# Prompt stick-breaking attention: every one-minus row on GpSimd, a second scan buffer for wide rows, q/k/v loads on the SyncE queue

## Chip, core, metric
One core of one Trainium2 chip runs the whole program. The metric is the device time of one execution in microseconds (us). Three timed runs gave 3248.36 to 3249.91 us, median 3248.76 us.

## What is computed
A two-layer decoder step for 1024 prompt tokens and 64 sample tokens. The change lies in the prompt part of layer 1, stick-breaking attention with 12 heads of 64:

```
z         = q k^T / 8 + bias[head]          (strictly causal)
log_keep  = where(mask, log_sigmoid(-z), 0)
log_after = reverse_cumsum(log_keep) - log_keep
a         = where(mask, exp(log_sigmoid(z) + log_after), 0)
out       = a v
```

So with b = sigmoid(z), a weight is b at its key times the product of (1 - b) over all later keys up to the query.

## The kernel before
The kernel is written engine by engine, with explicit semaphores; each engine runs its instructions in the written order. Layer 1 runs in this order: projections, prompt memory attention, sample memory attention, **prompt stick-breaking attention** ("the stage" below), sample stick-breaking attention, output projection, feed-forward.

The stage takes six head pairs and, for each, eight blocks of 128 queries in the order 0, 7, 1, 6, 2, 5, 3, 4: 48 steps. Block t has (t+1)*128 key columns. Odd steps (blocks 7 to 4) are *wide*, 640 to 1024 columns; even steps are *narrow*, 128 to 512. Step s works on two heads (`hh`), so there are 96 head rows.

In a step:
- TensorE (`pe_bp`): scores of step s+2 into PSUM, then for each *fill* of two key blocks the transposes of step s's weights (`turn`) and the product with v of the fill before (`use`). Only two PSUM banks (4 and 5) take fills, so TensorE and ScalarE hand them back and forth.
- ScalarE (`act_bp`): `breaks(s + 2)`, the sigmoid of the scores into `brk_w` or `brk_n`; for wide steps also sigmoid(-z) into `left_w`, chunk by chunk. Then it copies the turned fills of step s out of PSUM to `brk_t`.
- VectorE (`dve_bp`): for a narrow row first one-minus (`tensor_scalar`, brk_n to left_n); for every row the running product (`tensor_tensor_scan`, two inputs in SBUF: the `left` row and a broadcast zero), then the product with the breaks (`tensor_tensor`, two inputs in SBUF). `copy_out` subtracts PSUM and SBUF for the low half of the result.
- GpSimd (`pool_bp`): issues the loads. `raw(i)` brings q and k of pair i from DRAM (2 x 512 KB) into `sb_raw`, `values(i)` its v into `sb_v`. It waits for the end of the sample memory attention (`ms_lo`) before the first.
- `prep(i, m)`: TensorE transposes a quarter of `sb_raw`, ScalarE copies it to `sb_qk`. Pair 0's four are done ahead of the steps; the others inside steps 1 to 4 of the pair before.

`sp_ms` loads keys and values of the sample memory attention on the SyncE queue; `sp_bs` loads pages for the next stage.

Of the kernel before, what the change touches and what calls it, by code (L numbers as in the profile page):

```python
# [68 lines left out]
def build(nc, A, O, scratch):  # L69
    es = ExitStack()  # L70
    with es:
# [81 lines left out]
        nbias12 = r("nbias12", [P, SH])  # L153
# [8 lines left out]
        sb_raw = r("sb_raw", [P, 2, NPT, P])  # L162
# [3 lines left out]
        left_w = r("left_w", [P, 2, SEQ + 1])  # L166
        left_n = r("left_n", [P, 2, 512 + 1])
# [685 lines left out]
        def sig_after(n, hh):  # L853

            count = 0
            for s in range(NSTEP):
                for m, _, _ in chunks(s):
                    if m == n:
                        return count + (2 if wide(s) else 1) * (hh + 1)
                    count += 4 if wide(s) else 2  # L860
# [30 lines left out]
        sb_v = sb_at("sb_v", [P, 2, NPT, P], w_hi_at + (2 + idle_half) * half)  # L891

# [3 lines left out]
        def left_edge(s):  # L896
            return (left_w, SEQ) if wide(s) else (left_n, 512)
# [7 lines left out]
        def pool_bp(pool):  # L905

            pool.wait_ge(ms_lo, 4)
            def raw(i):
                for n in range(2):
                    pool.dma_start(sb_raw[:, n, :, :], proj[0:SEQ, n * MIX + i * P:n * MIX + (i + 1) * P]  # L910
                                   .rearrange("(t p) f -> p t f", p=P)).then_inc(bp_ld, 16)

            def values(i):
                pool.dma_start(sb_v[:, i % 2, :, :], proj[0:SEQ, 2 * MIX + i * P:2 * MIX + (i + 1) * P]
                               .rearrange("(t p) f -> p t f", p=P)).then_inc(bp_v[i % 2], 16)
# [108 lines left out]
        def act_bp(act):  # L1024
# [36 lines left out]
            act.wait_ge(bp_one, 4)  # L1061
# [13 lines left out]
        def dve_bp(dve):  # L1075
            dve.wait_ge(ms_lo, 4)
            dve.memset(left_w[:, :, SEQ:SEQ + 1], 1.0).then_inc(bp_one, 1)
            dve.memset(left_n[:, :, 512:513], 1.0).then_inc(bp_one, 1)
            dve.memset(zero1[:, :], 0.0).then_inc(bp_one, 1)
            dve.wait_ge(bp_set, 16)  # L1080
            dve.tensor_scalar(nbias12[:, :], bias12[:, :], -1.0, None, ALU.mult).then_inc(bp_one, 1)
            dve.wait_ge(bp_one, 4)
# [6 lines left out]
            for s in range(NSTEP):  # L1089
# [1157 lines left out]
```

## Time and profile before

| | us |
|---|---|
| median of the timed runs | 3248.76 |
| the profiled execution | 3256.13 |
| its span, first to last instruction | 3254.6 |
| mean granted TensorE clock | 0.961 of full |
| the stage, end of sample memory attention to last result | 1717.5 to 2025.7 |

The profile describes one execution, 7.4 us above the median. Its page gives busy time by engine, the chain that ended last, and the costliest groups. Since the page is a mean over stages with different limits, the change is read in the stage's own window. "Idle before, releaser" is the time that an engine stood still ahead of a group, and whose semaphore ended it.

### The profile page before, as it was taken

How to read it: one execution, taken by the hardware profiler on the slowest of the kernel's cores; microseconds unless marked ns; L12 is line 12 of the kernel's file. 1: busy time of each engine (PE TensorE's matmuls, PEld its weight loads, DVE VectorE, ACT ScalarE, POOL GpSimd, SP SyncE). 2: the span in 40 equal slices, each digit the busy share in tenths (PEclk: the TensorE clock that was granted, in tenths of full speed). 3: DMA queues.
4: the chain of work that ended last, by engine and by line, in shares of the span. 5: the costliest groups of instructions: out<-in, count | busy, mean ns of one | idle time of the engine just before them, and what ended most of it. 6: DMA issues, size and time to landing. Idle time of an engine off the chain costs nothing.

```text
span 3254.6 us, 52029 instructions
## 1 busy us (share of the span) xinstructions
PE 3009.7 (92%) x20232; PEld 2669.0 (82%) x20232; DVE 1758.9 (54%) x2649; ACT 1077.6 (33%) x1794; POOL 92.8 (3%) x163
## 2 busy tenths in 40 slices
PE   6996799999999999899966887999999999999997
PEld 6994699999999999799944444556899999999996
DVE  4016225666666666610035777555335666666666
ACT  5223223222222222522245666454133222222221
POOL 0010000000000000000001000000000000000000
PEclk8998899999999999899978889999999999999998
DMA  4122211111111111122242111999311111111101
GB/s 135 48 96 78 63 39 33 39 53 44 39 39 39 58 39 39 56 75 80 80 135 62 32 34 37 357 390 390 120 33 40 39 45 51 39 39 39 58 26 67
DMA packets 188140, 260.61 MB, mean 80 GB/s; under 512 B 9560, under 2 KB 138222, under 8 KB 188044
## 3 DMA queue, kind: packets, MB, share of 16 engines
q1 hardware_dynamic: 170752, 197.23, 17.6%
q0 software_dynamic: 16512, 61.71, 6.0%
q8 instruction: 67, 1.10, 0.1%
q10 hardware_dynamic: 780, 0.34, 0.0%
q14 instruction: 29, 0.24, 0.0%
HBM read 238.24 MB, written 27.68 MB: 82 GB/s over the span
## 4 chain that ended last, share of the span: by engine, by line
PE 80%; ACT 6%; DVE 5%; DMA 4%; issue 2%; SPq 2%; ACTq 0%; POOL 0%; DVEq 0%; POOLq 0%
PE ps L320 23%; PE ps L321 23%; PE ps L322 22%; DMA pv_tail<-in_cache_sb_v_dram 2%; PE ps L994 2%; PE ps L429 2%; ACT brk_w L1041 1%; ACT left_w L1046 1%; DVE x L1966 1%; PE ps L979 1%; PE ps L1217 1%; PE ps L964 1%; PE ps L1256 1%; PE ps L1234 1%; ACT prob L1585 1%
## 5 line engine op out<-in xcount | busy, mean ns | idle before, releaser
L1966 DVE TENSOR_TENSOR x<-x,ps 128x512 f32<-128x512 f32 (+1 forms) x792 | 538.9, 687 | 305.7 <-PE ps L322 304.8
L320 PE MATMUL ps<-act_hi,w_hi 128*128 128x370 f32 x2112 | 702.3, 333 | 1.4 <-DVE act_lo L464 1.4
L321 PE MATMUL ps<-act_lo,w_hi 128*128 128x370 f32 x2112 | 701.4, 332 | 0.0
L322 PE MATMUL ps<-act_hi,w_lo 128*128 128x370 f32 x2112 | 699.6, 331 | 0.0
L320 PE MATMUL ps<-w_hi,act_hi 128*128 128x256 f32 (+1 forms) x1800 | 507.2, 282 | 3.4 <-DVE w_lo L316 2.0
L321 PE MATMUL ps<-w_lo,act_hi 128*128 128x256 f32 (+1 forms) x1800 | 506.6, 281 | 0.0
L322 PE MATMUL ps<-w_hi,act_lo 128*128 128x256 f32 (+1 forms) x1800 | 505.0, 281 | 0.0
L320 PEld LDWEIGHTS ps<-act_hi,w_hi 128*128 128x128 f32 x2112 | 398.7, 189 | 5.7 <-DVE act_lo L464 1.7
L321 PEld LDWEIGHTS ps<-act_lo,w_hi 128*128 128x128 f32 x2112 | 398.5, 189 | 2.0
L322 PEld LDWEIGHTS ps<-act_hi,w_lo 128*128 128x128 f32 x2112 | 397.9, 188 | 0.0
L316 DVE TENSOR_TENSOR w_lo<-w_raw,w_hi 128x2048 fp32r<-128x2048 f32 x73 | 167.3, 2292 | 357.2 <-ACT w_hi L312 357.2
L320 PEld LDWEIGHTS ps<-w_hi,act_hi 128*128 128x128 f32 (+1 forms) x1800 | 330.5, 184 | 4.3 <-DVE w_lo L316 2.5
L322 PEld LDWEIGHTS ps<-w_hi,act_lo 128*128 128x128 f32 (+1 forms) x1800 | 330.8, 184 | 0.0
L321 PEld LDWEIGHTS ps<-w_lo,act_hi 128*128 128x128 f32 (+1 forms) x1800 | 330.8, 184 | 0.0
L320 PE MATMUL ps<-d_hi,g_hi 128*128 128x512 f32 (+1 forms) x792 | 310.9, 393 | 17.9 <-DVE d_lo L1901 17.9
L321 PE MATMUL ps<-d_lo,g_hi 128*128 128x512 f32 (+1 forms) x792 | 310.1, 392 | 0.0
L322 PE MATMUL ps<-d_hi,g_lo 128*128 128x512 f32 (+1 forms) x792 | 309.9, 391 | 0.0
L1933 ACT ACTIVATE g_hi<-cv_u 128x1024 fp32r<-128x1024 f32 x44 | 46.6, 1060 | 610.0 <-DVE cv_u L1980 610.0
L312 ACT ACTIVATE w_hi<-w_raw 128x2048 fp32r<-128x2048 f32 x73 | 138.9, 1902 | 163.9 <-PE ps L322 142.4
L1923 ACT ACTIVATE up_g<-ps 128x1110 f32<-128x1110 f32 x44 | 48.3, 1098 | 431.1 <-PE ps L322 431.1
L320 PEld LDWEIGHTS ps<-d_hi,g_hi 128*128 128x128 f32 (+1 forms) x792 | 144.9, 183 | 50.8 <-issue 18.9
L322 PEld LDWEIGHTS ps<-d_hi,g_lo 128*128 128x128 f32 (+1 forms) x792 | 145.0, 183 | 36.6
(288 smaller groups left out, 3645.7 us busy)
## 6 DMA issues: line engine op xcount, KB each, us to landing
w_raw<-in_w_up_dram SPq DMA_DIRECT2D x88, 512.0 KB, 4.9
pk_w<-in_cache_sb_k_dram SPq DMA_DIRECT2D x64, 384.0 KB, 5.3
pv_w<-in_cache_sb_v_dram SPq DMA_DIRECT2D x64, 384.0 KB, 5.3
pk_tail<-in_cache_sb_k_dram SPq DMA_DIRECT2D x64, 384.0 KB, 5.5
pv_tail<-in_cache_sb_v_dram SPq DMA_DIRECT2D x64, 384.0 KB, 5.4
d_raw<-in_w_down_dram POOLq DMA_DIRECT2D x44, 512.0 KB, 3.8
projected<-stage POOLq DMA_DIRECT2D x13, 1024.0 KB, 5.2
w_raw<-in_w_in_b_dram SPq DMA_DIRECT2D x20, 512.0 KB, 4.3
```

The source lines that it names most:

```text
L312: act.activation(w_hi[:, par], w_raw[:, :, :], ACT.Copy).then_inc(wh_ok, 1)
L316: dve.tensor_tensor(w_lo[:, par], w_raw[:, :, :], w_hi[:, par].bitcast(F32), ALU.subtract).then_inc(w_ok, 1)
L320: pe.matmul(out, ahi, bhi, start=first, stop=False, **kw)
L321: pe.matmul(out, ahi, blo, start=False, stop=False, **kw)
L322: return pe.matmul(out, alo, bhi, start=False, stop=last, **kw)
L429: last = pe.matmul(out, src(t, k), diag[0:ROWS[t], t, 0:ROWS[t]], start=True, stop=True, skip_group_check=True)
L964: last = pe.matmul(ps[:, 2 * (n % 2) + hh, 0:w], sb_qk[i % 2][rows, 0, t * P:(t + 1) * P], sb_qk[i % 2][rows, 1, c0:c0 + w], start=True, s ...
L979: last = pe.transpose(ps[:, 4 + n % 2, c:c + P], breaks_of(s)[:, hh, kb * P:(kb + 1) * P], ident[:, :])
L994: last = pe.matmul(ps[hh * HD:(hh + 1) * HD, 6 + s // 2 % 2, s % 2 * P:(s % 2 + 1) * P], sb_v[:, i % 2, kb, hh * HD:(hh + 1) * HD], brk_t[ ...
L1923: act.activation(up[:, :].rearrange("p (g c) -> p g c", c=TG), src, ACT.Copy)
L1933: act.activation(g_hi[:, par, 0:SEQ], cv_u[:, 2:2 + SEQ], ACT.Copy).then_inc(gh_ok, 1)
L1966: dve.tensor_tensor(xs, xs, ps[0:ROWS[t], DN_BANK[(2 * t + c) % 4], :], ALU.add).then_inc(dn_ev, 1)
```

## The change
1. ScalarE no longer computes sigmoid(-z). VectorE no longer computes one-minus. GpSimd computes 1 - b for all 96 head rows, from the finished break row in SBUF, into `left_w` or `left_n`; VectorE's scan waits for it (`bp_keep`).
2. `left_w` has two buffers, so a wide row may be written while the one before is in use; `left_n` keeps one. `nbias12` goes.
3. q, k, v loads move to the SyncE queue. Those of pair 0 are issued between the loads of the sample memory attention; `sb_raw` moves to the place of `w_raw`. TensorE starts `prep(0, 0)` after `ms_ok`, without waiting for the masks.
4. Page table, bias and masks are set up by GpSimd after the prompt memory attention (`mq_lo`). The first page load of the next stage goes behind the last `prep`; the load of `qkn_raw` behind the last scores, since it now lies over `sb_qk0`.

The diff's core, in the order of the file: buffers, `sp_bp`, `pool_bp`, `pe_bp`, `act_bp` (in `breaks`), `dve_bp`, `sp_bs`. `first` is called in `sp_ms` behind `load(mvc[0], ...)`; `sig_after(n, hh)` is now 2n + hh + 1.

```diff
-        left_w = r("left_w", [P, 2, SEQ + 1])
-        left_n = r("left_n", [P, 2, 512 + 1])
+        left_w = r("left_w", [P, 2, 2, SEQ + 1])
+        left_n = r("left_n", [P, 1, 2, 512 + 1])
+        sb_raw = sb_at("sb_raw", [P, 2, NPT, P], w_hi_at + 4 * half)
...
+            def first():
+                sp.wait_ge(w_ok, out0[1] + 1)
+                sp.wait_ge(w_used, out0[1])
+                raw(0)
+                values(0)
...
-            pool.wait_ge(ms_lo, 4)
...
+            pool.wait_ge(mq_lo, 2 + 16)
...
+            pool.wait_ge(ms_lo, 4)
+            for s in range(NSTEP):
+                w = (step(s)[1] + 1) * P
+                left, end = left_edge(s)
+                for hh in range(2):
+                    pool.wait_ge(bp_sig, sig_after(chunks(s)[-1][0], hh))
+                    ago = 4 if wide(s) else 2
+                    if s >= ago:
+                        pool.wait_ge(bp_a, 2 * (s - ago) + hh + 1)
+                    pool.tensor_scalar(left[:, hh, end - w:end], breaks_of(s)[:, hh, 0:w], -1.0, 1.0, ALU.mult,
+                                       ALU.add).then_inc(bp_keep, 1)
...
-            pe.wait_ge(ms_lo, 4)
-            pe.wait_ge(masked, BP_MASKED)
+            pe.wait_ge(ms_ok, 4)
...
-                        if wide(s):
-                            if s >= 2:
-                                act.wait_ge(bp_a, 2 * (s - 2) + hh + 1)
-                            act.activation(left[:, hh, at + c0:at + c0 + w], z, ACT.Sigmoid, bias=nbias12[:, h:h + 1],
-                                           scale=-1.0).then_inc(bp_sig, 1)
...
-                    dve.wait_ge(bp_sig, sig_after(chunks(s)[-1][0], hh))
-                    if not wide(s):
-                        dve.tensor_scalar(c, row, -1.0, 1.0, ALU.mult, ALU.add).then_inc(bp_keep, 1)
-                        dve.wait_ge(bp_keep, s + hh + 1)
+                    dve.wait_ge(bp_keep, 2 * s + hh + 1)
...
+            sp.wait_ge(bp_z, chunks((NPAIR - 1) * NPT - 1)[-1][0] + 1)
```

ScalarE in the first pair, from the breaks of step 2 to the first fill of step 1, before:

```order
L1041 ACTIVATE brk_n<-ps,bias_83 128x256 x2
L1053 ACTIVATE brk_t<-ps 128x256
L1041 ACTIVATE brk_w<-ps,bias_83 128x384
L1046 ACTIVATE left_w<-ps,nbias_84 128x384
L1041 ACTIVATE brk_w<-ps,bias_83 128x384
L1046 ACTIVATE left_w<-ps,nbias_84 128x384
L1041 ACTIVATE brk_w<-ps,bias_83 128x512
L1046 ACTIVATE left_w<-ps,nbias_84 128x512
L1041 ACTIVATE brk_w<-ps,bias_83 128x512
L1046 ACTIVATE left_w<-ps,nbias_84 128x512
L1053 ACTIVATE brk_t<-ps 128x512 x4
L1029 ACTIVATE sb_qk_151<-ps 128x512
```

The same place of the changed kernel:

```order
L1054 ACTIVATE brk_n<-ps,bias_83 128x256 x2
L1060 ACTIVATE brk_t<-ps 128x256
L1054 ACTIVATE brk_w<-ps,bias_83 128x384 x2
L1054 ACTIVATE brk_w<-ps,bias_83 128x512 x2
L1060 ACTIVATE brk_t<-ps 128x512 x4
L1044 ACTIVATE sb_qk_149<-ps 128x512
```

Four of eight activations between the narrow breaks and the fills are gone.

VectorE at its first steps (scans are listed as SCALAR_TENSOR_TENSOR), before:

```order
L1098 TENSOR_SCALAR left_n<-brk_n 128x128
L1100 SCALAR_TENSOR_TENSOR left_n<-left_n,zero_90 128x128
L1103 TENSOR_TENSOR brk_n<-brk_n,left_n 128x128
L1098 TENSOR_SCALAR left_n<-brk_n 128x128
L1100 SCALAR_TENSOR_TENSOR left_n<-left_n,zero_90 128x128
L1103 TENSOR_TENSOR brk_n<-brk_n,left_n 128x128
L1100 SCALAR_TENSOR_TENSOR left_w<-left_w,zero_90 128x1024
L1103 TENSOR_TENSOR brk_w<-brk_w,left_w 128x1024
```

The changed kernel:

```order
L1102 SCALAR_TENSOR_TENSOR left_n<-left_n,zero_89 128x128
L1105 TENSOR_TENSOR brk_n<-brk_n,left_n 128x128
L1102 SCALAR_TENSOR_TENSOR left_n<-left_n,zero_89 128x128
L1105 TENSOR_TENSOR brk_n<-brk_n,left_n 128x128
L1102 SCALAR_TENSOR_TENSOR left_w<-left_w,zero_89 128x1024
L1105 TENSOR_TENSOR brk_w<-brk_w,left_w 128x1024
L1102 SCALAR_TENSOR_TENSOR left_w<-left_w,zero_89 128x1024
L1105 TENSOR_TENSOR brk_w<-brk_w,left_w 128x1024
```

and GpSimd, which had nothing but loads there, now runs these beside it, twelve of each width in all:

```order
L947 TENSOR_SCALAR left_n<-brk_n 128x128 x2
L947 TENSOR_SCALAR left_w<-brk_w 128x1024 x2
L947 TENSOR_SCALAR left_n<-brk_n 128x256 x2
L947 TENSOR_SCALAR left_w<-brk_w 128x896 x2
L947 TENSOR_SCALAR left_n<-brk_n 128x384 x2
L947 TENSOR_SCALAR left_w<-brk_w 128x768 x2
L947 TENSOR_SCALAR left_n<-brk_n 128x512 x2
L947 TENSOR_SCALAR left_w<-brk_w 128x640 x2
```

VectorE has only the scan and the product of each row left; every scan now stands behind one of these rows.

SyncE in the sample memory attention of layer 1, changed kernel (before, the two rows in the middle were on GpSimd, behind the page table's load):

```order
L1667 DMA mkc<-in_cache_mem_k_dram 128x2x256 x4
L1667 DMA mvc_123<-in_cache_mem_v_dram 128x2x256 x4
L896 DMA sb_raw<-projected 128x8x128 x2
L900 DMA sb_v<-projected 128x8x128
L1667 DMA mvc_124<-in_cache_mem_v_dram 128x2x256 x4
L1667 DMA mkc<-in_cache_mem_k_dram 128x2x256 x4
```

Pair 0's three loads stand ahead of the second half of the sample group's memory loads.

## Rows read from the trace of the kernel before

**Rows 1.** The page: busy time by engine, and the chain that ended last.
```profile
PE 3009.7 (92%) x20232; PEld 2669.0 (82%) x20232; DVE 1758.9 (54%) x2649; ACT 1077.6 (33%) x1794; POOL 92.8 (3%) x163
...
PE 80%; ACT 6%; DVE 5%; DMA 4%; issue 2%; SPq 2%; ACTq 0%; POOL 0%; DVEq 0%; POOLq 0%
```

**Rows 2.** Stretch, length, busy PE, PEld, DVE, ACT, POOL; clock, DMA share, GB/s.
```profile
1640.00:1690.00 50.00, 31.13 (x257) 23.48 (x256) 26.79 (x47) 27.19 (x85) 0.00 (x0) 0.84 0.37 119
1717.50:2025.70 308.20, 244.42 (x1776) 143.77 (x1777) 227.61 (x269) 201.00 (x410) 18.90 (x27) 0.88 0.12 35
```

**Rows 3.** Waits in the stage: who for whom, total us, times, longest.
```profile
PE ps L994 <- ACT brk_t L1053: 46.3, 29, 2.5
...
DVE left_n L1098 <- ACT brk_n L1041: 28.7, 14, 3.7
...
DVE left_w L1100 <- ACT left_w L1046: 20.1, 12, 3.2
...
DVE act_lo L1087 <- ACT act_hi L1057: 13.8, 12, 3.2
```

**Rows 4.** Groups in the stage: busy us, mean ns; idle before, releaser.
```profile
L1100 DVE TENSOR_TENSOR_SCAN left_w<-left_w,zero 128x1024 f32<-128x1024 f32 (+3 forms) x48 | 90.8, 1891 | 21.4 <-ACT left_w L1046 20.1
...
L1046 ACT ACTIVATE left_w<-ps,nbias 128x512 f32<-128x512 f32 (+3 forms) x96 | 60.2, 627 | 3.3 <-DVE brk_w L1103 3.3
...
L1103 DVE TENSOR_TENSOR brk_w<-brk_w,left_w 128x1024 f32<-128x1024 f32 (+3 forms) x48 | 49.2, 1025 | 1.6
L1100 DVE TENSOR_TENSOR_SCAN left_n<-left_n,zero 128x128 f32<-128x128 f32 (+3 forms) x48 | 39.6, 825 | 1.7
...
L1103 DVE TENSOR_TENSOR brk_n<-brk_n,left_n 128x128 f32<-128x128 f32 (+3 forms) x48 | 23.6, 492 | 1.6
...
L1098 DVE TENSOR_SCALAR left_n<-brk_n 128x128 f32<-128x128 f32 (+3 forms) x48 | 15.6, 326 | 29.1 <-ACT brk_n L1041 28.7
...
L1087 DVE TENSOR_TENSOR act_lo<-ps,act_hi 128x256 fp32r<-128x256 f32 x24 | 10.2, 425 | 14.2 <-ACT act_hi L1057 13.8
```

**Rows 5.** The chain into the stage: start, us, what.
```profile
1716.18 1.08 PE ps L1772 x4
...
1717.54 0.24 DVE act_lo L1715
...
1718.56 0.92 POOL sb_raw L910
1719.48 5.84 DMA sb_raw<-projected
...
1725.46 3.76 PE ps L951 x16
```

**Rows 6.** VectorE at the stage's start and end: start, us, what, idle before.
```profile
1732.48 0.33 DVE L1098 TENSOR_SCALAR left_n<-brk_n 128x128 f32<-128x128 f32 x1 [3.67 <-ACT brk_n L1041]
...
1736.17 2.29 DVE L1100 TENSOR_TENSOR_SCAN left_w<-left_w,zero 128x1024 f32<-128x1024 f32 x1 [1.52 <-ACT left_w L1046]
1738.50 1.22 DVE L1103 TENSOR_TENSOR brk_w<-brk_w,left_w 128x1024 f32<-128x1024 f32 x1
...
2018.01 0.82 DVE L1103 TENSOR_TENSOR brk_w<-brk_w,left_w 128x640 f32<-128x640 f32 x1
```

**Rows 7.** TensorE's last wide scores of the stage, in order of time.
```profile
2011.21 1.13 PE L964 MATMUL ps<-sb_qk 64*128 64x512 f32 x4
```

**Rows 8.** GpSimd's instructions that read and write SBUF, by form, whole execution.
```profile
L746 POOL TENSOR_SCALAR_AFFINE_SELECT w_raw<-w_raw 128x768 f32<-128x768 f32 x1 | 0.9, 876 | 4.8 <-DMA w_raw<-in_gm_v_norm_dram 4.8
...
L337 POOL TENSOR_SCALAR_AFFINE_SELECT ident<-ident 128x128 f32<-128x128 f32 x1 | 0.3, 282 | 0.2 <-POOL batch_of L331 0.2
```

**Rows 9.** Layer 0: GpSimd and VectorE at the same moment, in order of time.
```profile
239.30 0.88 POOL L746 TENSOR_SCALAR_AFFINE_SELECT w_raw<-w_raw 128x768 f32<-128x768 f32 x1 [4.82 <-DMA w_raw<-in_gm_v_norm_dram]
...
239.34 1.64 DVE L803 SCALAR_TENSOR_TENSOR v_all<-v_all,inv,w_raw 128x768 f32<-128x768 f32 x1 [12.21 <-DMA w_raw<-in_gm_v_norm_dram]
```

**Rows 10.** All of line 803: duration ns, minimum, median, maximum.
```profile
L803 DVE SCALAR_TENSOR_TENSOR v_all<-v_all,inv,w_raw x9: 1000/1008/1644, 239.3 to 247.4; 128x768 f32<-128x768 f32 x8, 64x768 f32<-64x768 f32 x1
```

More of the change, by code:

```diff
@@ L853, in sig_after @@
         def sig_after(n, hh):
[L855 to L860, printed above, removed]
+            return 2 * n + hh + 1
         def blocks(s, f):
@@ L896, in left_edge, with sp_bp, raw, values @@
         def left_edge(s):
-            return (left_w, SEQ) if wide(s) else (left_n, 512)
+            return (left_w[:, s // 2 % 2], SEQ) if wide(s) else (left_n[:, 0], 512)
+        def sp_bp(sp):
+            def raw(i):
+                for n in range(2):
+                    sp.dma_start(sb_raw[:, n, :, :], proj[0:SEQ, n * MIX + i * P:n * MIX + (i + 1) * P]
+                                 .rearrange("(t p) f -> p t f", p=P)).then_inc(bp_ld, 16)
+            def values(i):
+                sp.dma_start(sb_v[:, i % 2, :, :], proj[0:SEQ, 2 * MIX + i * P:2 * MIX + (i + 1) * P]
+                             .rearrange("(t p) f -> p t f", p=P)).then_inc(bp_v[i % 2], 16)
+            def first():
[3 more added lines that the diff above has]
+                values(0)
+            def rest():
+                for i in range(1, NPAIR):
+                    sp.wait_ge(bp_t, prep_no(i - 1, 3) + 1)
+                    raw(i)
+                    if i >= 2:
+                        sp.wait_ge(bp_av, av_after((i - 1) * NPT - 1))
+                    values(i)
+            return first, rest
         def pool_sb_out(pool):
@@ L905, in pool_bp @@
         def pool_bp(pool):
-            pool.wait_ge(ms_lo, 4)
[L908 to L915, printed above, removed]
+            pool.wait_ge(mq_lo, 2 + 16)
             pool.dma_start(page_t[:, :], A["page_table"].rearrange("b p -> (b p)").unsqueeze(0)).then_inc(bs_set, 16)
-            raw(0)
-            values(0)
             pool.dma_start(bias12[:, :], A["sb_bias"][0].partition_broadcast(P)).then_inc(bp_set, 16)
@@ L1033, in breaks @@
                 i, t = step(s)
-                left, end = left_edge(s)
-                at = end - (t + 1) * P
                 for n, c0, w in chunks(s):
@@ L1076, in dve_bp @@
             dve.wait_ge(ms_lo, 4)
-            dve.memset(left_w[:, :, SEQ:SEQ + 1], 1.0).then_inc(bp_one, 1)
-            dve.memset(left_n[:, :, 512:513], 1.0).then_inc(bp_one, 1)
+            dve.memset(left_w[:, :, :, SEQ:SEQ + 1], 1.0).then_inc(bp_one, 1)
+            dve.memset(left_n[:, :, :, 512:513], 1.0).then_inc(bp_one, 1)
             dve.memset(zero1[:, :], 0.0).then_inc(bp_one, 1)
-            dve.wait_ge(bp_set, 16)
-            dve.tensor_scalar(nbias12[:, :], bias12[:, :], -1.0, None, ALU.mult).then_inc(bp_one, 1)
-            dve.wait_ge(bp_one, 4)
+            dve.wait_ge(bp_one, 3)
             dve.wait_ge(masked, BP_MASKED)
@@ L1185, in batch @@
                         new_values(b + 1)
-            keys(0, 0, pages(0, 0))
             page = [pages(0, g) for g in (0, 1, 2, 3)]
             sp.wait_ge(bp_t, prep_no(NPAIR - 1, 3) + 1)
+            keys(0, 0, page[0])
+            sp.wait_ge(bp_z, chunks((NPAIR - 1) * NPT - 1)[-1][0] + 1)
             sp.dma_start(qkn_raw[:, :, :], proj[SEQ:NTOK, 0:2 * MIX].rearrange("t (n f) -> t n f", n=2)).then_inc(bs_in, 16)
@@ L1657, in pe_mq, with sp_ms @@
             pe.wait_ge(mq_lo, 2 + 8 * (l + 1))
-        def sp_ms(sp, l):
+        def sp_ms(sp, l, then):
             def load(dst, name, gr):
@@ L1673, in sp_ms @@
             load(mvc[0], "cache_mem_v", 0)
+            if then:
+                then()
             sp.wait_ge(mq_nm, 9 * l + 9)
@@ L2072, in _ @@
                 load_cols(sp, out0[l], A["w_out"][l], 0)
-                sp_ms(sp, l)
+                pairs_first, pairs_rest = sp_bp(sp)
+                sp_ms(sp, l, pairs_first if l else None)
                 if l:
+                    pairs_rest()
                     sp_bs(sp)
```

13 lines of the change are left out of this document (2 added, 11 removed).

## The prediction, made before the changed kernel had run

> **What bounds the kernel now.** I read the page first. TensorE is busy 92% of the span, and four fifths of the chain that ended last are its [rows 1]. That is a mean: the change lies in one stage of 308 us. So next the stretches: there TensorE is busy 244 us, VectorE 228, ScalarE 201, at a granted clock of 0.88 of full [rows 2]. No engine is full; they wait for each other. The waits say how [rows 3]: TensorE stands 46.3 us for ScalarE's copies of turned fills (brk_t), because ScalarE does the eight activations of a wide step first. VectorE stands 28.7 us for narrow breaks, 20.1 for left_w, 13.8 for act_hi. So the stage is bound by the hand-over between TensorE and ScalarE, and VectorE has some 60 us to spare. Ahead of it, TensorE stands from 1717.3 to 1725.5 for the first load [rows 5].
>
> **Part 1: the first load.** TensorE's last matmul of the sample memory attention runs from 1716.18 and takes 1.08 us. GpSimd waits for the instruction behind it (1717.54), issues the page table and then sb_raw (1718.56), and this lands after 5.84 us; prep starts at 1725.46 [rows 5]. Afterwards these loads are issued ahead of or in the prompt memory attention, where the DMA engines are busy 37% [rows 2], and have some 50 us. TensorE's wait for ms_ok is met before its last matmul, so prep starts at 1717.26: 1725.46 - 1717.26 = **-8.2 us**. It all lies on the chain. What would be late next is the bias and the masks; GpSimd sets them up during the sample memory attention now, so nothing. The two sample loads queued behind the three new issues on SyncE wait for semaphores of the sample memory attention anyway: nothing. The other moves cost nothing as long as their cover holds: qkn_raw is loaded after the last scores (2011.21 + 1.13 = 2012.3 [rows 7]) and used at the stage's end, 2025.7, and sb_raw, a larger load, took 5.84 us; the page load behind the last prep goes out earlier still. If that cover went, the excess would fall on the start of the next stage, a few us.
>
> **Part 2: what leaves ScalarE and VectorE.** ScalarE loses 96 activations, 60.2 us [rows 4], in each pair 10 us. Their worth is not 60 us: TensorE's wait for ScalarE is 46.3 us [rows 3], and when that is gone TensorE has nothing left to wait for. So relief of ScalarE gives at most **-46.3 us**. VectorE loses 48 narrow one-minus, 15.6 us [rows 4].
>
> **Part 3: what GpSimd adds.** 96 rows; the columns of a pair are 2 x (1+...+8) x 128 = 9216, of six pairs 55296. No row shows GpSimd's tensor_scalar. The nearest is its affine select, also one input and one output: 876 ns for 768 columns, 282 ns for 128 [rows 8], that is 0.928 ns a column and 163 ns fixed. So 55296 x 0.928 + 96 x 163 ns = 51.3 + 15.6 = **67.0 us** (0.28 us for the narrowest row, 1.11 for the widest). Bounds: as fast as VectorE's one-minus, 0.33 us mean for a narrow row [rows 4], it would be about half; at one and a half times the select's time it would be 100 us. I take the select.
>
> **Part 4: the two engines do not run side by side.** In layer 0 the trace has one meeting. GpSimd's select ran from 239.30 for 0.88 us, to 240.18; VectorE started an instruction with two SBUF inputs at 239.34, and that took 1.644 us, where the median of its line is 1.008 [rows 9, 10]. It ended at 240.98, 0.80 us behind GpSimd's end. So it stood for the whole rest of GpSimd's instruction, and only 0.20 us of its own start was hidden behind it. All of VectorE's scans and products in this stage have two SBUF inputs. I therefore add GpSimd's rows to VectorE's time, not beside it.
>
> The Trainium skill has this as a rule ("SBUF — State Buffer", section "Who interferes with whom"): a VectorE instruction with two SBUF inputs contends with a GpSimd instruction that reads SBUF, through one shared pair of ports that is held for the whole instruction. By that rule, the meeting in layer 0 agrees, 0.64 us longer. It speaks against this change: without it part 3 would cost nothing.
>
> VectorE and GpSimd as one resource: scans 90.8 + 39.6, products 49.2 + 23.6, copy-outs 10.2 = 213.4 us [rows 4]. Two hand-overs a row of about 0.035 us (a scan from 1736.17, 2.29 long, its product at 1738.50 [rows 6]) are 6.7: 220.1. GpSimd adds 67.0 at most, and 96 x 0.20 = 19.2 less if each row hides as much as in layer 0: 47.8. Sum 267.9 to 287.1, middle 277.5. To that 3 us for the start, where the two widest rows (2 x 1.11) both stand ahead of the first wide scan: **280.5**. Before, VectorE's stretch from its first row to its last product is 1732.48 to 2018.83 = 286.35 us [rows 6], waits included. So **-5.9 us**. This holds only if VectorE, now the slowest, rarely waits for the rest. I expect so: TensorE and ScalarE alone need 286.35 - 46.3 = 240 us. And after a wide step VectorE has a narrow and a wide step ready, about 10 us, about as long as fills, prep and next breaks take. The tail behind the last product (6.9 us) stays.
>
> **Sum.** -8.2 - 5.9 = -14.1 us. The profiled execution, 3256.1, would be 3242.0; against the median, which is 7.4 lower, 3248.8 - 14.1 = 3234.7, so **3235 us**. With the ends of the stretch (270.9 and 290.1 with the start's 3 us) its own range is -23.7 to -4.5, and some us for the waits: 3224 to 3246.
>
> **Rivals.**
> - *No mutual exclusion in this stage.* Then VectorE needs 220 us, hides inside the 240 of TensorE and ScalarE, and the ceiling of part 2 counts: say four fifths of 46.3, since a row still passes through GpSimd, 37. With the load -45: 3204 us. For it: only one meeting is in the trace. Against: that one is plain.
> - *The gain is eaten by waits that stay.* Exclusion as above, and because GpSimd's row steps in between scan and product, each step's weights come later, TensorE and ScalarE start its fills later and the narrow breaks after them come late too. VectorE waits 56 us now besides the end; if 15 of it stays on top of the full resource, +9 in the stage, and with the load +1: 3249 us. For it: half of VectorE's wait is for narrow breaks, which come behind fills.
> - *Slower: GpSimd's tensor_scalar takes longer than its select.* At one and a half times, rows of 100.5 us, 81.3 with the hidden part: 220.1 + 81 to 100 + 3 = 304 to 324, against 286.35 +18 to +37, with the load +10 to +29: 3268 us. It decides from where the rows cost 286.35 + 8.2 - 220.1 - 3 = 71.5 us besides what is hidden, so 0.74 us to 0.94 us a row on the mean where the select gives 0.70. For it: arithmetic in two steps where the select has a compare. Against: the select reads and writes as many columns.
>
> The Trainium skill gives for GpSimd loops ("GPSIMD Engine Reference", section "3.1 Elementwise — side-by-side cycle accounting") 1.03 cycles a column when the body has one or two operations, at 1.2 GHz 0.86 ns; by it part 3 would be an estimated 63 us and the sum 4 us better. The same section measured 1.8 cycles for a longer loop, an estimated 99 us, which would be the slower rival. No row here tells the two apart; the select's 0.928 ns is near the first.
>
> **Chances.** Forecast 0.54, of which a sixth lies within the resolution; no exclusion 0.12; waits stay 0.16; slow rows 0.18. A measurement of this kernel tells about 0.2%, 6.5 us, from no change. Faster 0.45 + 0.12 + 0.03 of the third case = 0.60; within 0.2% 0.09 + 0.13 = 0.22; slower 0.18. For 8 in 10 the range takes in the third case and the near part of the fourth, and half of the way to the second: 3214 to 3260.
>
> **What the profile after would show.** Prep starts within 1 us of the last sample matmul, and the stage's first breaks about 8 us earlier: part 1. GpSimd's 128x1024 row at about 1.1 us, 67 us in all: part 3. Scans and products longer on the mean than now (1.89 and 1.03 us for wide rows), by together 48 to 67 us over the stage: part 4; unchanged durations would mean the first rival. TensorE's wait for brk_t far under 46 us, and VectorE's waits short: the forecast; VectorE's waits above 15 us: the second rival. GpSimd's mean row above 0.9 us: the third. The prediction is wrong if the stage shrinks by more than 30 us or grows.

## The result, and the profile after

The changed kernel takes 3210.5 us (median; 3205.5 to 3212.5) beside 3249.3 us of the kernel before on the same chip: ratio 0.9879, interval 0.9857 to 0.9902, so -38.9 us. On a second chip it took 3210.5 beside 3248.9 (0.9892, 0.9871 to 0.9912). The prediction said 3235, with a range of 3214 to 3260: the direction was right, the size much too small.

The page after, busy time and chain, answers to [rows 1]. VectorE's share of the chain is 8% where it was 5%, and GpSimd is in it:

```profile
PE 2995.9 (93%) x20232; PEld 2662.5 (83%) x20232; DVE 1769.7 (55%) x2600; ACT 1034.7 (32%) x1698; POOL 181.8 (6%) x241
...
PE 77%; DVE 8%; issue 6%; DMA 3%; ACT 2%; SPq 2%; POOL 2%; ACTq 0%; DVEq 0%; POOLq 0%
```

Two stretches (columns as in [rows 2]): the stage from the last result of the sample memory attention to its own last result, and in it VectorE's stretch from its first scan to its last product.

```profile
1718.40:1986.65 268.25, 228.94 (x1785) 135.08 (x1784) 238.85 (x222) 156.96 (x313) 105.18 (x96) 0.93 0.12 35
1724.26:1979.82 255.56, 219.14 (x1710) 128.57 (x1706) 237.07 (x214) 150.55 (x302) 104.75 (x95) 0.93 0.11 33
```

The same two stretches of the first profile of before, the second from its first narrow one-minus:

```profile
1717.54:2026.38 308.84, 245.10 (x1787) 144.45 (x1788) 228.23 (x271) 200.99 (x409) 18.90 (x27) 0.88 0.12 35
1732.48:2018.83 286.35, 232.85 (x1690) 135.89 (x1690) 226.29 (x262) 193.38 (x396) 11.42 (x13) 0.89 0.10 29
```

VectorE's stretch is 30.8 us shorter, not 5.9. (A second profile of before, in the table below, has 279.7 us for it, so some of the 30.8 can be the one execution.) In it VectorE is busy 237.1 of 255.6 us, idle 18.5 where it was 60.1. TensorE's busy time in it fell as well, 232.9 to 219.1 for the same matmuls, at a granted clock of 0.93 in place of 0.89. Who waits now (answers to [rows 3]):

```profile
ACT brk_t L1060 <- PE ps L993: 67.2, 57, 6.8
PE ps L993 <- DVE brk_w L1105: 27.4, 7, 7.0
DVE left_n L1102 <- POOL left_n L947: 9.2, 7, 5.5
DVE left_w L1102 <- POOL left_w L947: 8.6, 6, 1.6
PE ps L1008 <- ACT brk_t L1060: 7.2, 17, 0.8
DVE act_lo L1092 <- ACT act_hi L1064: 5.1, 1, 5.1
```

TensorE's wait for ScalarE's brk_t went from 46.3 to 7.2 us. A new wait of 27.4 us stands in its place, for VectorE's products. The groups (answers to [rows 4]) show that VectorE's instructions became longer: wide scans 90.8 to 100.6, narrow scans 39.6 to 46.0, products 49.2 to 54.2 and 23.6 to 28.8 us.

```profile
L1102 DVE TENSOR_TENSOR_SCAN left_w<-left_w,zero 128x1024 f32<-128x1024 f32 (+3 forms) x48 | 100.6, 2095 | 10.1 <-POOL left_w L947 8.6
...
L947 POOL TENSOR_SCALAR left_w<-brk_w 128x1024 f32<-128x1024 f32 (+3 forms) x48 | 60.7, 1281 | 50.7 <-ACT brk_w L1054 50.7
L1105 DVE TENSOR_TENSOR brk_w<-brk_w,left_w 128x1024 f32<-128x1024 f32 (+3 forms) x48 | 54.2, 1129 | 1.6
...
L1102 DVE TENSOR_TENSOR_SCAN left_n<-left_n,zero 128x128 f32<-128x128 f32 (+3 forms) x48 | 46.0, 958 | 9.9 <-POOL left_n L947 9.2
L947 POOL TENSOR_SCALAR left_n<-brk_n 128x128 f32<-128x128 f32 (+3 forms) x48 | 44.6, 945 | 126.9 <-ACT brk_n L1054 126.9
L1105 DVE TENSOR_TENSOR brk_n<-brk_n,left_n 128x128 f32<-128x128 f32 (+3 forms) x48 | 28.8, 600 | 1.6
```

The stage's start, in order of time, answers to [rows 5, 6]:

```profile
1717.47 0.63 PE L1775 MATMUL ps<-pick,ms_out 128*128 128x32 f32 x4 [0.57 <-DVE ms_out L1713]
1717.94 1.07 PE L965 MATMUL ps<-ident,sb_raw 128*128 128x128 f32 x8
...
1723.83 0.56 POOL L947 TENSOR_SCALAR left_n<-brk_n 128x128 f32<-128x128 f32 x2 [33.38 <-ACT brk_n L1054]
...
1724.26 0.42 DVE L1102 TENSOR_TENSOR_SCAN left_n<-left_n,zero 128x128 f32<-128x128 f32 x1 [5.49 <-POOL left_n L947]
...
1725.90 2.06 POOL L947 TENSOR_SCALAR left_w<-brk_w 128x1024 f32<-128x1024 f32 x2 [1.50 <-ACT brk_w L1054]
```

Prep starts with the last sample matmuls, where it stood 8.2 us. VectorE stands still while the first row of each pair runs, so these show GpSimd's own duration: 0.29 us for 128 columns, 1.05 for 1024 (the pairs take 0.56 and 2.06), close to the select's 0.28 and 1.11.

### The profile page after: what moved, and what is told of

Read it like the earlier page. It is cut to its first block, busy times and chain, and to the rows that moved or that the text cites. A ratio compares the mean times of both kernels' runs of the same rounds, so it can differ in the third digit from the quotient of the medians.

```text
span 3209.4 us, 52070 instructions
## 1 busy us (share of the span) xinstructions
PE 2995.9 (93%) x20232; PEld 2662.5 (83%) x20232; DVE 1769.7 (55%) x2600; ACT 1034.7 (32%) x1698; POOL 181.8 (6%) x241
## 4 chain that ended last, share of the span: by engine, by line
PE 77%; DVE 8%; issue 6%; DMA 3%; ACT 2%; SPq 2%; POOL 2%; ACTq 0%; DVEq 0%; POOLq 0%
PE ps L318 23%; PE ps L319 23%; PE ps L320 23%; PE ps L427 2%; DMA pv_tail<-in_cache_sb_v_dram 2%; DVE x L1969 1%; DVE left_w L1102 1%; PE ps L1218 1%; DVE brk_w L1105 1%; SPq L1156 1%; POOL left_w L947 1%; PE ps L1257 1%; POOL left_n L947 1%; SPq L1165 1%; ACT prob L1586 1%
## 5 line engine op out<-in xcount | busy, mean ns | idle before, releaser
L318 PE MATMUL ps<-d_hi,g_hi 128*128 128x512 f32 (+1 forms) x792 | 310.9, 393 | 17.9 <-DVE d_lo L1904 17.9
L1936 ACT ACTIVATE g_hi<-cv_u 128x1024 fp32r<-128x1024 f32 x44 | 46.6, 1060 | 611.2 <-DVE cv_u L1983 611.2
```

Source lines behind the costliest of these rows:

```text
L318: pe.matmul(out, ahi, bhi, start=first, stop=False, **kw)
L1936: act.activation(g_hi[:, par, 0:SEQ], cv_u[:, 2:2 + SEQ], ACT.Copy).then_inc(gh_ok, 1)
```

## The experiments

After the result, two theories of the stage were put against each other. **A**: VectorE and GpSimd are one resource, which sets the end; a row of GpSimd costs about its columns. **B**: the exclusion hardly matters, the gain is ScalarE's relief. What is called *growth* below is VectorE's busy time in its stretch over 210.7 us, which is what scans, products and copy-outs take there undisturbed (226.3 of before less 15.6 for the narrow one-minus [rows 4]).

| kernel | us, median | ratio to before | stretch, us | VectorE growth, us | VectorE idle, us | clock |
|---|---|---|---|---|---|---|
| before | 3249.3 | | 286.4 | 0 | 60.1 | 0.89 |
| before, second profile | | | 279.7 | 0 | 53.5 | 0.91 |
| changed | 3210.5 | 0.9879 | 255.6 | 26.4 | 18.5 | 0.93 |
| changed, second chip | 3210.5 | 0.9892 | 255.9 | 26.3 | 19.0 | 0.93 |
| loads only | 3246.6 | 0.9987 | 286.0 | 0 | 59.9 | 0.89 |
| loads only, again | 3243.0 | 0.9985 | 287.9 | 0 | 61.7 | 0.89 |
| one wide buffer | 3211.2 | 0.9894 | 255.9 | 26.1 | 19.1 | 0.93 |
| narrow rows on ScalarE | 3231.0 | 0.9945 | 275.8 | 20.1 | 45.0 | 0.88 |
| ScalarE's load back | 3238.4 | 0.9963 | 283.0 | 21.9 | 50.4 | 0.91 |
| GpSimd's rows twice | 3228.2 | 0.9938 | 273.9 | 51.3 | 11.9 | 0.92 |
| GpSimd only writes | 3199.9 | 0.9836 | 241.2 | -0.2 | 30.6 | 0.96 |
| rows in halves | 3202.5 | 0.9843 | 249.8 | 13.3 | 25.7 | 0.94 |
| rows in halves, again | 3206.4 | 0.9873 | 249.7 | 13.5 | 25.5 | 0.94 |
| pieces of 256 | 3208.1 | 0.9883 | 255.5 | 6.7 | 38.1 | 0.93 |

Stretch, growth, idle and clock are of the one profiled execution of each kernel, which can lie up to 9 us from its median (that of the pieces of 256 is 8.6 us under, that of the narrow rows on ScalarE 9.2 over). The growth and the stretch of the changed kernel repeat within 0.4 us, the stretch of before only within 7. Each ratio is to runs of before on the same chip; the runs lie on four chips, so ratios are compared between them, not times.

**The loads alone.** Loads, their set-up and the start of prep as changed; one-minus as before:

```diff
-                    pool.tensor_scalar(left[...], breaks_of(s)[:, hh, 0:w], -1.0, 1.0, ALU.mult, ALU.add)
+                        if wide(s):
+                            act.activation(left[...], z, ACT.Sigmoid, bias=nbias12[...], scale=-1.0)
+                    if not wide(s):
+                        dve.tensor_scalar(c, row, -1.0, 1.0, ALU.mult, ALU.add)
```

> Only the loads, their set-up and the start of prep are as in the changed kernel; ScalarE's and VectorE's one-minus rows are those of the kernel before, GpSimd makes none. Both theories of the stage agree here, since neither speaks of loads: 8.2 us for the first load and some tenths after it, so about 3240 us beside 3249 of the kernel before (ratio 0.9972). The VectorE stretch (first row to last product) stays at 286 us. Then the 30 us that are left belong to the one-minus rows. Rival: the load's 8 us is not seen at the end, 3248, and the rows are worth nearly 39. The stage after this one was 5.7 us shorter in the changed kernel's profiled run: if that comes from the moved loads it shows here too (3234), if it is from run to run it does not.

> Only the loads moved, once more, with more rounds, since the first interval (0.9965 to 1.0009) holds both answers. If the first load is worth its 8.2 us at the end: 3241, ratio 0.9975 with the upper end under 1. If something gives it back: 3247 or more, ratio 0.999 and above.

Measured 0.9987 (0.9965 to 1.0009) and 0.9985 (0.9970 to 0.9999). The second is -4.9 us, with an interval from -9.7 to -0.3. Over both chips, 22 runs beside 36, the means differ by 4.4 us, with 3.4 as twice the standard error: 1.0 to 7.8 us. In the trace the gap is gone:

```profile
1720.97 0.63 PE L1783 MATMUL ps<-pick,ms_out 128*128 128x32 f32 x4 [0.57 <-DVE ms_out L1721]
1721.43 3.63 PE L960 MATMUL ps<-ident,sb_raw 128*128 128x128 f32 x16
```

and the stage, from the end of the sample memory attention to its own last result, takes 297.2 and 300.2 us, where the two profiles of before have 308.6 and 302.4. So the 8.2 us are there in place; at the end 4 to 5 are seen. Each interval alone still holds 8.2, the two taken together end just under it. Some 34 of the 39 us are left for the rows.

**Before, once more.**

> The kernel before, a second profiled execution. It tells which stretches differ from run to run without any change: the first profile was 7 us over the median. If the stage itself takes 308 us again and the stage behind it 270 us in place of 275, the 5.7 us behind the stage are not from the change.

The stage took 302.4 us, not 308, and what lies behind it 1228.3 us, as in the first profile (1228.2). The 1222.8 of the changed kernel's first profile is the lowest of all 14 profiles, which go up to 1231.4 in no order that follows the edits (1226.4 in the changed kernel's second one, 1231.4 in the loads alone). So the 5.4 us between the two first profiles need not be from the change.

**One wide buffer.**

```diff
-        left_w = r("left_w", [P, 2, 2, SEQ + 1])
+        left_w = r("left_w", [P, 1, 2, SEQ + 1])
-                    ago = 4 if wide(s) else 2
+                    ago = 2
```

> The changed kernel with one left_w buffer in place of two. Theory A (VectorE and GpSimd are one resource in this stage, it sets the end, and a row of GpSimd costs it about its columns, some 32 us over 96 rows, since the fixed parts of both are hidden behind the other's instruction): a row starts later but costs the same; it waits for the product of the wide row two steps before, which is usually done, so 0 to +6 us, 3211 to 3217. Theory B (the exclusion hardly matters for the end; the gain is ScalarE's relief, and what is left is hand-overs): the second buffer takes hand-overs away, so without it +5 to +15, 3216 to 3226. Rival C, that the second buffer is where most of the unforeseen gain is from: +20, 3231.

3211.2 us, stretch 255.9: the second buffer brings nothing that can be measured. Rival C falls. A's range holds it; the time lies under B's (3216 to 3226), but the interval of the ratio, 0.9858 to 0.9931, is too wide to decide between them.

**Narrow rows on ScalarE.** In `breaks`, while GpSimd skips these rows:

```diff
+                        if not wide(s):
+                            act.activation(left[:, hh, end - w:end], z, ACT.Sigmoid, bias=nbias12[...],
+                                           scale=-1.0).then_inc(bp_sig, 1)
```

> The changed kernel, but ScalarE makes the one-minus of the 48 narrow rows (15360 of 55296 columns) straight from the scores, some 0.3 to 0.6 us each, 22 us in all; GpSimd keeps the 48 wide rows. Theory A: the pair of VectorE and GpSimd loses 15360 x 0.928 ns = 14 us and the hand-over ScalarE, GpSimd, VectorE of the narrow rows, so -8 to -14 us: about 3200. Theory B: ScalarE's 22 us stand ahead of fills, so +5 to +15: about 3221.

Ratio 0.9945 beside 0.9879, 21 us slower than the changed kernel, though growth fell by 6 us. A alone is wrong. B has the sign, but its +5 to +15 is less than was measured. The cause in the trace: ScalarE does four activations for the narrow breaks of the next step before its copies of the fills, and TensorE has nothing to do until they come. ScalarE, then TensorE, in the same step:

```profile
1850.36 0.69 ACT L1062 ACTIVATE brk_n<-ps,bias 128x512 f32<-128x512 f32 x1 [0.68 <-PE ps L990]
1850.94 0.68 ACT L1067 ACTIVATE left_n<-ps,nbias 128x512 f32<-128x512 f32 x1
1851.52 0.69 ACT L1062 ACTIVATE brk_n<-ps,bias 128x512 f32<-128x512 f32 x1
1852.08 0.70 ACT L1067 ACTIVATE left_n<-ps,nbias 128x512 f32<-128x512 f32 x1
1852.65 0.89 ACT L1074 ACTIVATE brk_t<-ps 128x512 f32<-128x512 f32 x2
```

```profile
1851.07 0.44 PE L1001 MATMUL ps<-ident,brk_n 128*128 128x128 f32 x2
1853.41 1.12 PE L1016 MATMUL ps<-brk_t,sb_v 128*64 128x128 f32 x8 [1.91 <-ACT brk_t L1074]
1854.46 1.12 PE L973 MATMUL ps<-ident,sb_raw 128*128 128x128 f32 x4
```

The prep that stands behind it took 1.12 us for 4, where the three others of each pair take 0.66 in that run, and everything on TensorE is slower for some us. Two stretches around this wait (columns as in [rows 2]) show it: the granted clock is 1.00 ahead of it and 0.50, the lower of its two levels, behind it.

```profile
1846.00:1851.00 5.00, 5.00 (x46) 2.95 (x42) 4.90 (x4) 2.33 (x6) 0.56 (x1) 1.00 0.00 0
...
1853.40:1856.00 2.60, 2.59 (x16) 1.94 (x16) 0.52 (x1) 0.52 (x2) 0.00 (x0) 0.50 0.00 0
```

Over the whole stretch the clock is 0.88, and TensorE's busy time 233.8 where the changed kernel has 219.1. So a wait seems to be paid twice. This profile is of the slowest of its ten runs, 9 us over their median, so some of its stretch is that run's own. VectorE's waits for the copies (act_hi) rose from 5.1 to 17.8 us, for left_w from 8.6 to 23.5. ScalarE's copies (brk_t) waited 61.6 us for TensorE in this same stage: its slack lies elsewhere.

**ScalarE's load back.** The kernel with one wide buffer, and 96 activations into a spare tile:

```diff
+                        if wide(s):
+                            act.activation(ghost[:, ghosts[0] % 4, 0:w], z, ACT.Sigmoid, bias=bias12[...],
+                                           scale=-1.0).then_inc(ghost_ok, 1)
```

> The kernel with one left_w buffer, and in addition ScalarE still does the 96 activations sigmoid(-z) of the wide rows (60 us), into a spare tile that nobody reads; GpSimd makes all 96 rows. Control: the same without them. Theory A (VectorE and GpSimd as one resource set the end): ScalarE waits 67 us for TensorE in the changed kernel, so most of this hides: 0 to +12 us over its control. Theory B (the gain is ScalarE's relief): all of the 30 us in the stage is gone, +30 or more, 3241 and above.

Ratio 0.9963 beside its control's 0.9894, 22 us, and stretch 283.0 beside 255.9: nearly the whole gain of that stretch is gone. A (0 to +12) has missed; B has the mechanism, but its size (+30 or more) is more than was measured. TensorE's old wait is back, and VectorE has its growth of 21.9 us besides:

```profile
PE ps L1011 <- ACT brk_t L1069: 42.0, 27, 2.5
DVE left_w L1111 <- POOL left_w L950: 32.0, 14, 4.6
DVE left_n L1111 <- POOL left_n L950: 15.3, 12, 5.5
```

**GpSimd's rows twice.**

```diff
+                    pool.tensor_scalar(ghost[:, hh, 0:w], breaks_of(s)[:, hh, 0:w], -1.0, 1.0, ALU.mult,
+                                       ALU.add).then_inc(ghost_ok, 1)
```

> The kernel with one left_w buffer, each GpSimd row done twice, first into a spare tile. 96 more rows, 55296 more columns, 67 us of GpSimd's own time. Theory A (the columns count, fixed parts are hidden): at least +51 us over its control less what falls into VectorE's waits (about 20), so +31 to +51, 3245 to 3265. If only 0.20 us of VectorE's start is hidden a row, as in my forecast, +48 to +67. Theory B (GpSimd is beside the path): each row comes later by its own length but only the first of a step is waited for, 0 to +15.

Ratio 0.9938 beside 0.9894, 14 us; stretch 273.9, +18.0. GpSimd's own time grew by 67 us, VectorE's growth by 25.2 and of that 18 reached the end. The two intervals of the ratio overlap a little (0.9858 to 0.9931, 0.9913 to 0.9962), so the sizes are better taken from the stretch. A has missed: its price of a row is more than twice too high. B's range (0 to +15) holds the 14 us, but not for its reason: VectorE does not wait longer for later rows, it idles less (11.9 us in place of 19.1), and its own instructions grow. So it is the bound here.

**GpSimd only writes.** A memset in place of the row, so that the weights come from a constant and this kernel leaves out the one-minus:

```diff
-                    pool.tensor_scalar(left[...], breaks_of(s)[:, hh, 0:w], -1.0, 1.0, ALU.mult, ALU.add)
+                    pool.memset(left[:, hh, end - w:end], 0.5)
```

> The changed kernel with GpSimd's row replaced by a memset of the same columns to 0.5: it writes SBUF and reads none. This leaves out the one-minus (its values are constants), so the output is not the reference's. Theory A: VectorE's scans and products are back at their own durations if it is the read that shuts VectorE out (wide 90.8 and 49.2, narrow 39.6 and 23.6 in place of 100.6, 54.2, 46.0, 28.8), so VectorE needs 26 us less and the next limit is TensorE with ScalarE: 3190 to 3200. If the writing shuts it out as well, durations and time stay, 3205 to 3211. Theory B: the time stays, whatever the durations do.

Ratio 0.9836 beside the changed kernel's 0.9879, 14 us, as A said and not B; stretch 241.2. Every scan and product is back at its own duration:

```profile
L1101 DVE TENSOR_TENSOR_SCAN left_w<-left_w,zero 128x1024 f32<-128x1024 f32 (+3 forms) x48 | 90.8, 1892 | 17.8 <-POOL left_w L947 16.5
...
L1104 DVE TENSOR_TENSOR brk_w<-brk_w,left_w 128x1024 f32<-128x1024 f32 (+3 forms) x48 | 49.2, 1026 | 1.6
L1101 DVE TENSOR_TENSOR_SCAN left_n<-left_n,zero 128x128 f32<-128x128 f32 (+3 forms) x48 | 39.4, 820 | 11.8 <-POOL left_n L947 11.2
L947 POOL MEMSET left_w<- 128x1024 f32 (+3 forms) x48 | 36.7, 793 | 75.4 <-ACT brk_w L1053 75.4
```

So it is GpSimd's reading of SBUF that stretches VectorE, not its writing. The Trainium skill ("SBUF — State Buffer", section "Who interferes with whom") says just that, and the trace agrees, with 0 us of growth beside 26.4. The stretch without any growth is 241.2 us, and VectorE idles 30.6 in it: so near is the limit that TensorE and ScalarE set. TensorE itself is not full there: it is busy 215.0 us and stands 16.0 for VectorE's products.

```profile
1728.46:1969.61 241.15, 214.99 (x1712) 126.34 (x1710) 210.52 (x214) 151.03 (x302) 53.81 (x95) 0.96 0.12 35
...
PE ps L992 <- DVE brk_w L1104: 16.0, 7, 5.5
```

Two things besides the reading differ in this kernel and were not tested apart: the memset is shorter (793 ns on the mean for a wide row, beside some 880 of an undisturbed one-minus), and TensorE multiplies other values.

**Rows in halves.**

```diff
+                    for o in (0, w // 2):
+                        pool.tensor_scalar(left[:, hh, end - w + o:end - w + o + w // 2],
+                                           breaks_of(s)[:, hh, o:o + w // 2], ...).then_inc(bp_keep, 1)
```

> The changed kernel with each GpSimd row done in two instructions of half the columns: 192 instead of 96 instructions, the same 55296 columns. This asks which part of a row costs. Theory A (the fixed 163 ns of a GpSimd instruction is hidden behind VectorE's running one): 0 to +5 us, 3211 to 3216. Rival, the sum of my forecast: the fixed part counts, +15.6 us less what is hidden, +8 to +16, 3219 to 3227.

> The kernel with each GpSimd row in two halves once more, on the same chip as the changed kernel: whether the 8 us between them hold. By the law above (13.3 us of growth in place of 26.4, and a little over half of a growth reaches the end) 6 to 8 us under the changed kernel; rival: it was the chip, 0 to 2.

3202.5 and, on another chip, 3206.4: faster, where both the theory and its rival had expected no gain from the first run. Twice as many instructions of GpSimd over the same columns halve VectorE's growth, 26.4 to 13.3. So part of every GpSimd instruction costs VectorE nothing, and more instructions save more. The second run lies between what was expected of it and its rival: 4.1 us under the changed kernel by the medians, 6.2 by the means.

```profile
L1104 DVE TENSOR_TENSOR_SCAN left_w<-left_w,zero 128x1024 f32<-128x1024 f32 (+3 forms) x48 | 96.4, 2009 | 16.0 <-POOL left_w L948 14.9
...
L1104 DVE TENSOR_TENSOR_SCAN left_n<-left_n,zero 128x128 f32<-128x128 f32 (+3 forms) x48 | 40.8, 851 | 13.0 <-POOL left_n L948 12.6
```

**Pieces of 256 columns.** The same with `for o in range(0, w, 256)`, 240 instructions.

> The changed kernel with GpSimd's rows done in pieces of at most 256 columns: 240 instructions in place of 96, the same columns. Law to be tested, from the runs so far: VectorE's scans and products grow by GpSimd's own duration less about 0.4 us for each GpSimd instruction (26.4 us over 96 rows, 51.3 over 192, 13.3 over 192 halves). A piece of 256 columns is 256 x 0.928 + 163 = 0.40 us, so by the law the growth is 0 to 4 us, and the stretch goes towards the 241 us of the kernel whose GpSimd only writes: 243 to 249, so 3193 to 3200. Rival: GpSimd waits for VectorE's running instruction ahead of each piece, so that a 1024 row comes after four of them, 4 to 6 us, and VectorE waits for it: growth small as well, but waits for GpSimd of 30 us and more in place of 18, stretch 250 to 260, 3203 to 3213.

Growth fell once more, to 6.7 us (the law had said 0 to 4), and the stretch went back to 255.5: the rival is right. VectorE's waits for GpSimd rose from 17.8 to 40.4 us:

```profile
DVE left_w L1105 <- POOL left_w L948: 27.2, 40, 2.5
DVE left_n L1105 <- POOL left_n L948: 13.2, 13, 7.2
```

In order of time, GpSimd and VectorE at the two widest rows of a pair:

```profile
1799.86 6.01 POOL L948 TENSOR_SCALAR left_w<-brk_w 128x256 f32<-128x256 f32 x8 [2.44 <-ACT brk_w L1056]
1801.56 2.40 DVE L1105 TENSOR_TENSOR_SCAN left_w<-left_w,zero 128x1024 f32<-128x1024 f32 x1 [1.47 <-POOL left_w L948]
1804.00 1.23 DVE L1108 TENSOR_TENSOR brk_w<-brk_w,left_w 128x1024 f32<-128x1024 f32 x1
...
1805.97 2.40 DVE L1105 TENSOR_TENSOR_SCAN left_w<-left_w,zero 128x1024 f32<-128x1024 f32 x1 [0.74 <-POOL left_w L948]
```

Eight pieces, 3.2 us of work, take 6.01: a piece that meets a running scan waits for its end. The sixth starts at 1801.80 and takes 2.37 us in place of 0.40, to 1804.17; the scan ends at 1803.96. The second row is ready only 0.7 us after the product is done.

**The changed kernel again.**

> The changed kernel once more, beside the pieces, the halves and the loads alone: 3206 to 3214 us.

3210.5. The halves are 4.1 us below it on the same chip; their intervals (0.9852 to 0.9895, 0.9871 to 0.9912) overlap. The stretch is 6 us shorter in both profiles of the halves than in the three of the changed kernel and its one-buffer form. The halves are the fastest version found that computes the result, by 4 to 8 us; the end alone does not settle it beyond doubt.

## Why the prediction was wrong

By its own sign (the stage shrinks by more than 30 us) the prediction is wrong: the stage went from 308.8 to 268.3 us. Its four parts, one by one:

*Part 1, the first load.* Right in place: prep starts within the last sample matmuls. At the end the two measurements of the loads alone give -4.2 and -4.9 us for a forecast of -8.2; each interval holds it, the two together (-1.0 to -7.8) just do not. Whether the rest is given back is open. It is not in the memory attention whose loads now share the queue: from its softmax table load to its last result the profiles of before have 79.8 and 84.5 us, those of the loads alone 76.4 and 82.1, though SyncE took 7.38 and 6.04 us to issue sb_raw there, 15.00 and 16.83 to issue sb_v.

*Part 2, ScalarE's relief.* The mechanism was right: with the load put back the stretch returns to 283.0. That the ceiling came out to a microsecond was luck. It was 286.35 - 46.3 = 240 us for TensorE and ScalarE alone, and the kernel whose GpSimd only writes, and so has no growth, has 241.2. But TensorE did not run out of waits, as the prediction had it: it idles 26.2 us there, where it idled 53.5 before, 27.3 less. The other 17.9 us are its own busy time, 232.9 to 215.0, at a granted clock of 0.96 in place of 0.89, which the prediction did not have at all. And with the second profile of before the same sum gives 279.7 - 46.6 = 233.

*Part 3, GpSimd's rows.* The price of one row was right (0.29 and 1.05 us seen, 0.28 and 1.11 predicted). So was the 67 us, within 5%: the shortest row of each width, added up over all 96, gives 64.0. In the profile the rows take 105.3 us, 1.10 on the mean, and by the prediction's own sign (a mean above 0.9) that would be the slow-row rival. The sign was badly chosen, since a row that stands for VectorE counts as long as it stands; the undisturbed rows show that this rival fell.

*Part 4, the two engines side by side.* The mechanism was right, and reading is the cause of it. The size is the step that failed. I charged VectorE with 47.8 to 67.0 us, and took the middle, 57.4; the growth measured is **26.4 us**. The stretch as measured is 210.7 (own) + 26.4 (growth) + 6.2 (hand-overs) + 12.3 (waits for rows inside it, 9.2 + 8.6 - 5.5) = 255.6. My other terms were 213.4 (the last copy-out, outside the stretch, and small overlaps in it), 6.7 and 3. So the rows are 31.0 us of the error, and the waits, 9.3 more than the 3 allowed for them, took part of it back.

Where the error lies: I charged VectorE with every row in full, less 0.20 us of its own start, from the one meeting in layer 0 [rows 9]. There GpSimd ran first and VectorE came 0.04 us behind it, so GpSimd had nothing to hide behind. In that order the stage shows the same price: GpSimd's second wide row starts at 1726.91 and takes 1.05 us, and the scan 0.14 us behind it takes 3.04 in place of 2.29, so 0.16 us is hidden.

```profile
1727.05 3.04 DVE L1102 TENSOR_TENSOR_SCAN left_w<-left_w,zero 128x1024 f32<-128x1024 f32 x1 [1.26 <-POOL left_w L947]
```

But mostly it is the other way round here: of the 95 rows in the stretch 73 start while a scan or product runs. Such a meeting of the changed kernel, in order of time:

```profile
1817.05 2.37 DVE L1102 TENSOR_TENSOR_SCAN left_w<-left_w,zero 128x1024 f32<-128x1024 f32 x1
1818.48 3.54 POOL L947 TENSOR_SCALAR left_w<-brk_w 128x896 f32<-128x896 f32 x2 [1.20 <-ACT brk_w L1054]
1819.45 1.77 DVE L1105 TENSOR_TENSOR brk_w<-brk_w,left_w 128x1024 f32<-128x1024 f32 x1
1821.26 1.30 DVE L1102 TENSOR_TENSOR_SCAN left_n<-left_n,zero 128x256 f32<-128x256 f32 x1
```

GpSimd's row of 896 columns (0.99 us of its own) starts at 1818.48 while the scan runs to 1819.42, and can read only then. The product behind it takes 1.77 us, 0.55 over its own 1.22; the next scan 1.30, 0.61 over the 0.69 it takes alone. Two rows of 0.99 us cost VectorE 1.16 together, and 0.41 a row is hidden. Over all runs the part of one GpSimd instruction that is not charged is its own time (an estimate by the prediction's 0.928 ns a column and 163 ns) less the growth. The last column says how much of it is no hiding: GpSimd's work at times when VectorE stands still or copies out (in the changed kernel 13.6 us, of which 12.7 stand still):

| kernel | GpSimd instructions | own us | growth, us | not charged, each | of it beside no scan or product |
|---|---|---|---|---|---|
| changed | 96 | 67.0 | 26.4 | 0.42 | 0.14 |
| rows twice | 192 | 134.0 | 51.3 | 0.43 | 0.11 |
| halves | 192 | 82.6 | 13.3 | 0.36 | 0.13 |
| pieces of 256 | 240 | 90.4 | 6.7 | 0.35 | 0.15 |
| wide rows alone | 48 | 44.9 | 20.1 | 0.52 | 0.27 |

It goes more with the number of instructions than with the columns. Some 0.20 to 0.33 us of each instruction is hidden behind VectorE's on the mean, 0.41 in the meeting above, where GpSimd comes second, and the rest fell into VectorE's idle time. So the forecast was wrong twice here: it had only the order with the small hiding, and it charged VectorE also with the 13.6 us of rows that ran beside none of its scans and products. Pieces of 256 columns (0.40 us) hardly lengthen VectorE's instructions, but they are not free: VectorE waits for them. That the 0.41 is made of the two fixed parts, some 0.20 of VectorE and 0.16 of GpSimd, each behind the other's instruction, is an argument from these numbers; no run separates them.

*The price at the end.* From 241.2 the growth of 26.4 brings the stretch to 255.6: 14.4, a little over half; the next 25.2 bring 18.0. I had VectorE as the only bound and so charged all of it. In fact TensorE and ScalarE at 241 and VectorE at about 237 are near each other, and a wait of one hides the growth of the other in part. The rival without exclusion had this ceiling too, but its mechanism is refuted; its time, 3204, came nearer than mine by luck, because a growth of 26 costs little. The second rival (waits that stay) came in part: VectorE idles 18.5 us in the stretch, above the 15 that were its sign, and its waits inside are 9.3 us over what I had allowed. But they lie in a stretch that is not full, so the time did not come out near 3249.

Theory A, that this pair alone is the bound, has fallen with the narrow rows on ScalarE (20 us slower with less growth); theory B, that the exclusion does not matter, with the constants (-14, some of which may be the memset's shorter duration) and with the stretch of the doubled rows (+18.0, with VectorE waiting less). What stands is both: in the profiled stretch the relief of ScalarE, with VectorE's narrow one-minus gone, is worth 45 us (286.35 to 241.2; 38.5 from the second profile of before), and GpSimd's rows with the exclusion take back 14.

## What to carry to other kernels

Moving work from an engine in the hand-over chain to GpSimd can pay although GpSimd and VectorE shut each other out: what it cost VectorE in this stage was not GpSimd's duration, but that less about 0.4 us for each instruction, part of it hidden and part done while VectorE stood still. So bound such a price from both ends, one that charges the whole duration and one that lets the fixed parts of both engines hide, do not take it from one meeting in which only one of the two orders occurs, and leave out the work that runs while the other engine waits. Cutting the rows once moved VectorE's growth down faster than its waits up; cutting them again gave it all back. And slack of an engine is worth nothing at the place where another waits for it: ScalarE's copies wait 67 us for TensorE in this stage, and 25 us more work ahead of its copies cost 20 (0.9945 beside 0.9879 is 21).

## What the runs showed of the hardware

- GpSimd's memset to SBUF did not lengthen VectorE's two-input scans and products at all (90.8, 49.2, 39.4, 23.6 us beside 90.8, 49.2, 39.6, 23.6); its tensor_scalar, which reads SBUF, did by 26.4 us. It holds for the scan with a broadcast zero as second input.
- The exclusion goes both ways: a VectorE scan of 2.29 us took 3.04 beside a GpSimd row that had started 0.14 us earlier, and a GpSimd piece of 0.40 us took 2.37 beside a running scan.
- 36 runs of the unchanged kernel on two of the chips go from 3234 to 3261 us. In the profiles this spread is partly in the two memory attentions. The two profiles of before have 79.8 us there at a granted clock of 0.82, and 84.5 at 0.72, with TensorE busy 52.8 and 60.1 us; those of the loads alone 76.4 at 0.84 and 82.1 at 0.75. The two ends of all profiles are the pieces of 256, whose loads there differ, and the second one of before:

```profile
1630.41:1704.82 74.41, 50.07 (x374) 37.89 (x375) 32.13 (x69) 35.71 (x104) 2.44 (x9) 0.87 0.43 139
```

```profile
1631.26:1715.79 84.53, 60.06 (x370) 44.20 (x370) 32.13 (x69) 36.35 (x104) 0.00 (x0) 0.72 0.32 104
```

- Fewer waits in the stage went with a higher granted clock of the same stretch: 0.89 and 0.91 in the two profiles of before, 0.93 changed, 0.96 with constants, and TensorE's busy time for nearly the same matmuls was 232.9 and 225.4, then 219.1 and 215.0 us. The clock there is either full or half: by it, TensorE has 63.0 us of its busy time at the lower level in the first profile of before, 28.5 changed and 18.8 with constants. So of the 45 us between before and the constants some 18 came back through TensorE itself, not as waits. That the shorter waits are what kept the clock up is not shown by these sums; the one wait followed above, 1.91 us with the clock at 1.00 before and 0.50 after, points that way.
